# Hybrid encoder trunk: gate and branch products with tokens as the stationary side, 512 weight columns moving

## The reference

```
h = rms_norm(x, norm1_g[l])
(aq, ak, av, bq, ..., c_q, c_kv, k_rope) = split(h @ w_in[l])
...                                              # o_a, o_b, o_c, o_d: four attentions
br = stack([o_a, o_b, o_c, o_d], axis=2)         # 256 channels each
y = einsum('bsnc,ncd->bsnd', br, w_branch[l])
g = sigmoid(h @ w_gate[l] + b_gate[l]).reshape(B, S, 4, D)
x = x + sum(g * y, axis=2) @ w_o[l]
h2 = rms_norm(x, norm2_g[l])
x = x + square(relu(h2 @ w_ff1[l])) @ w_ff2[l]
```

## Time and profile before

| | |
|---|---|
| median of 3 runs | 831.93 us (831.73 to 832.6) |
| profiled execution, its time | 832.6 us |
| its span | 830.8 us |
| TensorE busy | 816.9 us, 5763 products |
| VectorE busy | 544.4 us, 805 instructions |
| ScalarE busy | 409.6 us, 698 instructions |
| GpSimd busy | 45.7 us |
| transfers | 141.09 MB, 170 GB/s on average |
| granted TensorE clock | 1.00 in every slice |

### The profile page before, as it was taken

One profiled execution on the slowest core, in us unless ns is written; L12 is line 12 of the kernel. 1 busy time (PEld: TensorE's weight loads), 2 busy tenths in 40 slices (PEclk: granted clock), 3 DMA queues, 4 the chain that ended last, 5 costly groups with the idle time before them and its releaser, 6 DMA issues.

```text
span 830.8 us, 14799 instructions
## 1 busy us (share of the span) xinstructions
PE 816.9 (98%) x5763; PEld 749.1 (90%) x5763; DVE 544.4 (66%) x805; ACT 409.6 (49%) x698; POOL 45.7 (5%) x81
## 2 busy tenths in 40 slices
PE   7999999999999999999999999999999999999996
PEld 6999979999899999999899999799988999999995
DVE  6687676865776665555767675687665865555663
ACT  6356655655454444333464475575545544333442
POOL 1420000000010000000013100000000100000000
PEclk9999999999999999999999999999999999999999
DMA  8976534536347555566546755334353665566541
GB/s 248 227 233 198 158 120 135 150 105 204 101 156 237 169 174 178 200 202 199 170 128 194 241 167 177 116 102 153 126 177 104 212 199 178 197 202 198 170 137 50
DMA packets 100851, 141.09 MB, mean 170 GB/s; under 512 B 4797, under 2 KB 87041, under 8 KB 100801
## 3 DMA queue, kind: packets, MB, share of 16 engines
q1 hardware_dynamic: 99296, 137.12, 52.1%
q0 software_dynamic: 1216, 3.17, 1.7%
q10 hardware_dynamic: 288, 0.11, 0.1%
HBM read 139.33 MB, written 1.05 MB: 169 GB/s over the span
## 4 chain that ended last, share of the span: by engine, by line
PE 93%; DVE 3%; ACT 1%; issue 1%; POOL 1%; DMA 1%; POOLq 0%; ACTq 0%; DVEq 0%
PE bank_w L1190 20%; PE bank_w L1192 19%; PE bank_w L1191 19%; PE bank_acc L1190 8%; PE bank_acc L1191 8%; PE bank_acc L1192 8%; PE bank_acc L1286 2%; PE bank_o L1315 2%; PE bank_acc L1298 2%; DVE w_lo L810 2%; DMA cst<-in_table 1%; PE bank_x L1263 0%; PE bank_x L1268 0%; POOL rstd L498 0%; PE bank_x L1259 0%
## 5 line engine op out<-in xcount | busy, mean ns | idle before, releaser
L810 DVE TENSOR_TENSOR w_lo<-raw,w_hi 128x1024 fp32r<-128x1024 f32 (+1 forms) x256 | 309.0, 1255 | 49.6 <-ACT w_hi L575 49.5
L1190 PE MATMUL bank_w<-act_hi,w_hi 128*128 128x256 f32 x1008 | 287.9, 286 | 0.0
L1192 PE MATMUL bank_w<-act_hi,w_lo 128*128 128x256 f32 x1008 | 285.8, 283 | 0.0
L1191 PE MATMUL bank_w<-act_lo,w_hi 128*128 128x256 f32 x1008 | 285.2, 283 | 0.0
L575 ACT ACTIVATE w_hi<-raw 128x1024 fp32r<-128x1024 f32 (+1 forms) x256 | 257.0, 1060 | 26.7 <-DMA raw<-in_w_gate 12.9
L1190 PEld LDWEIGHTS bank_w<-act_hi,w_hi 128*128 128x128 f32 x1008 | 191.6, 190 | 6.9 <-ACT big L696 3.5
L1191 PEld LDWEIGHTS bank_w<-act_lo,w_hi 128*128 128x128 f32 x1008 | 190.9, 189 | 1.8 <-issue 0.5
L1192 PEld LDWEIGHTS bank_w<-act_hi,w_lo 128*128 128x128 f32 x1008 | 191.2, 190 | 0.0
L704 ACT ACTIVATE part_hi<-big 128x512 fp32r<-128x512 f32 x32 | 20.3, 633 | 194.2 <-DVE big L1038 191.5
L1190 PE MATMUL bank_acc<-w_hi,part_hi 128*128 128x512 f32 x256 | 100.3, 392 | 0.0
L1191 PE MATMUL bank_acc<-w_lo,part_hi 128*128 128x512 f32 x256 | 100.3, 392 | 0.0
(11 more groups left out here) (180 smaller groups left out, 938.5 us busy)
## 6 DMA issues: line engine op xcount, KB each, us to landing
raw<-in_w_ff SPq DMA_DIRECT2D x128, 512.0 KB, 4.7
raw<-in_w_gate SPq DMA_DIRECT2D x64, 512.0 KB, 4.7
raw<-in_w_in SPq DMA_DIRECT2D x32, 536.0 KB, 5.5
raw<-in_w_o SPq DMA_DIRECT2D x16, 512.0 KB, 4.5
raw<-in_w_branch SPq DMA_DIRECT2D x16, 256.0 KB, 4.5
raw<-in_w_branch SPq DMA_DIRECT2D x8, 512.0 KB, 4.6
xs<-in_x SPq DMA_DIRECT2D x2, 512.0 KB, 4.6
out_y<-big SPq DMA_DIRECT2D x4, 256.0 KB, 2.1
```

The lines of the kernel that those rows point to most:

```text
L810: nc.vector.tensor_tensor(half_view(w_lo, c, hf), raw_half(c, hf), f32(half_view(w_hi, c, hf)), ALU.subtract).then_inc(w_lo_ready, 1)
L1190: nc.tensor.matmul(dst, s_hi, m_hi, start=first, stop=False)
L1191: nc.tensor.matmul(dst, s_hi, m_lo, start=False, stop=False)
L1192: ins = nc.tensor.matmul(dst, s_lo, m_hi, start=False, stop=last)
```

## The change

**Gates.** Two gate chunks form a group of 512 features: chunk 2g holds the first half of the inner dimension, 2g+1 the second. The tokens become the stationary side, and 512 weight columns move. The group takes both banks, one for each half of the tokens; the sums run over both chunks. Gate weights are loaded in rows of 512 columns.

**Bias.** A feature is now a column, so the bias is a row. GpSimd broadcasts 512 biases to all partitions for each group (`gate_row`, two buffers). VectorE adds it from PSUM into `big` (`gate_add`): for the first token half as soon as TensorE's semaphore `gate_first` tells of it in the middle of the odd chunk, for the second at the end of the step. TensorE waits for these additions, and ScalarE's tanh, in `big` itself, comes behind them. The bias columns are gone from `vec_all`.

**Branches.** Quarters are now (token half, 512 features), 6 products of 128x512 each. The first comes behind gate 7 instead of 6, the third behind 13 instead of 12.

**Mixture.** `mix` has tokens on partitions now, so TensorE transposes it (16 transposes of 128x128 a layer), and ScalarE and VectorE read the turned quarters from PSUM. VectorE's split of `w_o` chunk 2 moves behind the last branch.

```diff
-Y_AFTER = {3 * n + 6: n for n in range(NB - 1)}
+Y_AFTER = {7: 0, 9: 1, 13: 2}
+GROUPS = GATE_N // 2
...
@@ SP: loads @@
+                if kind == "gate":
+                    k = KD // 2 * (i % 2) + 2 * h
+                    src = w_gate.rearrange("l (k p) (c n) -> l c p k n", p=P, n=512)[l, i // 2]
+                    sp.dma_start(dst.rearrange("p (k n) -> p k n", k=2), src[:, k:k + 2, :]).then_inc(done, 16)
...
@@ GpSimd @@
+            def gate_bias(l, g):
+                row = b_gate[bass.ds(l, 1), g * 512:(g + 1) * 512]
+                pool.dma_start(gate_row[:, g % 2, :], row.to_broadcast([P, 512])).then_inc(gate_row_landed[g % 2], 16)
...
                 norm(2 * l, l)
+                pool.wait_ge(gate_read, l * GATE_N)
+                for g in range(2):
+                    gate_bias(l, g)
...
+                for g in range(2, GROUPS):
+                    pool.wait_ge(gate_read, l * GATE_N + 2 * (g - 1))
+                    gate_bias(l, g)
                 norm(2 * l + 1, l)
...
@@ ScalarE, gate(i, l) @@
+                g = i // 2
+                if i % 2 == 0:
+                    return
+                for t in range(T):
+                    z = gate_slot(g // 2, 2 * t + g % 2)
+                    act.wait_ge(gate_read, l * GATE_N + (2 * g + t + 1))
+                    nc.scalar.activation(z, z, ACT.Tanh, scale=0.5).then_inc(gate_tanh, 1)
...
@@ VectorE @@
+            def gate_add(i, t, l):
+                g = i // 2
+                if i % 2 == 0:
+                    return
+                if t == 0:
+                    dve.wait_ge(gate_row_landed[g % 2], 16 * (l * GROUPS // 2 + g // 2 + 1))
+                    dve.wait_ge(gate_first, l * GROUPS + (g + 1))
+                else:
+                    dve.wait_ge(w_used, used_count(l, POS["gate", i]))
+                nc.vector.tensor_tensor(gate_slot(g // 2, 2 * t + g % 2), bank_w[:, t, :], gate_row[:, g % 2, :],
+                                        ALU.add).then_inc(gate_read, 1)
...
@@ TensorE @@
-                    pe.wait_ge(gate_tanh, l * GATE_N + (n + 1))
+                    pe.wait_ge(gate_read, l * GATE_N + (2 * n + q + 1))
...
+            def gate(i, l):
+                g, half = divmod(i, 2)
...
+                for t in range(T):
+                    tok = slice(t * P, (t + 1) * P)
+                    if half == 0:
+                        bank_free(("gate", g, t), l)
...
+                    ins = split_product(bank_w[:, t, :], sides, half == 0, half == 1)
+                    if half and t == 0:
+                        ins.then_inc(gate_first, 1)
+                ins.then_inc(w_used, 1)
...
+            def turn_mix(q, l):
+                pe.wait_ge(mixed, l * 12 + (8 + q + 1))
+                for j in range(KD // 2):
+                    ins = nc.tensor.transpose(mix_banks[q][:, j * P:(j + 1) * P], mix[:, q, j * P:(j + 1) * P], ident)
+                ins.then_inc(mix_turned, 1)
+            def last_branch(l):
+                for q in range(3):
+                    branch_part(NB - 1, q, l)
+                turn_mix(0, l)
+                branch_part(NB - 1, 3, l)
+                turn_mix(1, l)
...
@@ w_o_sums @@
+                    if c == 0:
+                        turn_mix(2, l)
+                        turn_mix(3, l)
```

More of the change, by code:

```diff
@@ L75 @@
 W_JOBS = []
-for _i in range(GATE_N):
-    W_JOBS.append(("gate", _i, 0))
-    if _i in Y_AFTER:
-        W_JOBS += [("y", Y_AFTER[_i], q) for q in range(4)]
+for _g in range(GROUPS):
+    W_JOBS += [("gate", _g, t) for t in range(T)]
+    if 2 * _g + 1 in Y_AFTER:
+        W_JOBS += [("y", Y_AFTER[2 * _g + 1], q) for q in range(4)]
 W_JOBS += [("y", NB - 1, q) for q in range(4)]
@@ L315, in trunk_kernel @@
         x_evac = sem("x_evac")
+        gate_row_landed = [sem(f"gate_row_landed{b}") for b in range(2)]
+        gate_first = sem("gate_first")
+        gate_read = sem("gate_read")
         gate_tanh = sem("gate_tanh")
@@ L689, in gate, with mix_hi @@
             def gate(i, l):
-                act.wait_ge(w_used, used_count(l, POS["gate", i]))
-                if i >= 8:
-                    act.wait_ge(y_read, l * 16 + (i - 7))
-                bank = bank_w[:, W_AT["gate", i, 0] % 2, :]
-                for d in range(2):
-                    ins = nc.scalar.activation(big[:, i % 8, d * SEQ:(d + 1) * SEQ], bank[:, d * SEQ:(d + 1) * SEQ],
-                                               ACT.Tanh, bias=vec(BG + 2 * i + d, l), scale=0.5)
-                ins.then_inc(gate_tanh, 1)
+                g = i // 2
[5 more added lines that the diff above has]
+                    nc.scalar.activation(z, z, ACT.Tanh, scale=0.5).then_inc(gate_tanh, 1)
+            def mix_hi(q, l):
+                t, m = divmod(q, 2)
+                kcs = slice(m * KD // 2, (m + 1) * KD // 2)
+                act.wait_ge(mix_turned, l * 4 + (q + 1))
+                nc.scalar.activation(act_hi[:, kcs, t * P:(t + 1) * P], mix_banks[q].rearrange("p (k s) -> p k s", s=P),
+                                     ACT.Copy, scale=0.5).then_inc(mix_hi_ready, 1)
             def mlp(i, l, g=0):
@@ L1075, in _ @@
                         branch(j, l, (0, 1))
+                    if kind == "gate":
+                        gate_add(j, 0, l)
                     if kind == "in":
@@ L1094, in _ @@
                             split_lo(c, l)
+                    if kind == "gate":
+                        gate_add(j, 1, l)
                     if s == 8:
```

86 lines of the change are left out of this document (46 added, 40 removed).

## The result

| | before | after |
|---|---|---|
| median on the same chip, 4 runs each | 832.1 us (831.73 to 832.6) | 847.6 us (846.3 to 849.25) |
| ratio, 95% interval | | 1.0188 (1.0172 to 1.0203) |
| span of the profiled execution | 830.8 us | 846.6 us |
| mean granted TensorE clock | 1.00 | 0.992 |
| products and transposes on TensorE | 5763 | 4835 |

The account below looks back on a forecast made before the run. TensorE, busy 98% of the span, was taken as the bound. Products, transposes and old waits gave -7.2 us, new waits +19.8, bias rows +0.5: +13.1, so 845.0 us on the median, range 833 to 852 for 8 in 10.

Parts of the forecast that it names:

- transposes and excursions: Turning the mixture: 16 transposes a layer, 1.86 us, plus three excursions into and out of small work, 0.6; 4.9 us more.
- place 1: Gate 1 to gate 2: TensorE waits for banks that VectorE's additions free late; 4.5 us lost in each layer.
- place 2: Step 15 to 16: k/v up-projection waits for ScalarE's copy behind the second addition and tanh; 1.8 us lost a layer.
- place 3: Step 18 to 19: first k transposes wait for ScalarE's copy behind late addition and tanh; 2.5 us lost a layer.
- place 4: Gate 13 to branch 2: VectorE reads the first quarter late, TensorE wants its bank for the third; 1.1 us a layer.
- bias rows and head: GpSimd's first two bias broadcasts of layer 0 compete with late weight loads; cost between 0 and 2.3 us, taken as 0.5.
- 40 x 0.28: 16 gate and 4 branch chunks per layer turn wide, each saving the MLP stage's 0.28 us: 11.2 us less.
- The rival that rests on the Trainium skill's figure: Gates and branches: each product saved is worth only 2.5 ns, so the gain is 2.4 us: 853.8; chance 0.02.
- M: End of a step's maxima on VectorE; 75.23 in step 9, with the second addition ending at M + 6.66.
- The covers hold: Rival: the second addition is nowhere wanted before it is done, so no new waits: 824.7 us; chance 0.13.
- only place 1 bites: Rival: queues behind the other three places are shorter than reckoned, only gate 2 waits: 834.2 us; chance 0.15.
- Lateness carries on: Rival: ScalarE's waits delay later work, other group borders lose too, bias rows cost 2.3; waits 26 us: 853; chance 0.15.

Follow-up runs that it names:

- halves beside the split last: 832 of the 960 wide products done as two of 256 columns, against the version with the split last (833.3 us): 840.05 us, ratio 1.0098.
- the split last: VectorE's weight split put behind normalising and second addition in every gate step, against the kernel after the change: 833.32 us, ratio 1.0011 to the kernel before.
- kept-busy run: 24 identity transposes on TensorE during its wait before gate 2's second token half, against the kernel after the change: 843.06 us, ratio 1.0127.
- tuned version: Against the split last: step 9's first addition and branch 1's first two reads ahead of maxima, `w_o` chunk 1's split behind the last branch: 843.65 us.
- additions in a row: VectorE's second addition straight behind the first, split and normalising after both, against the kernel after the change: 836.93 us, ratio 1.0058.
- transposes doubled beside the tuned version: Each of the mixture's 32 transposes done twice, against the tuned version: 843.85 us, ratio 1.0138.
- short rows: Each half chunk of gate weights loaded as two loads of 256 columns (1 KB pieces), against the kernel after the change: 847.52 us, ratio 1.0176.

## Why the prediction was right

The direction, the place and the mechanism held: 847.6 lies in the forecast's own 840 to 850, and the waits are at the four places named. Moving the second addition takes back nearly all of the loss, and moving only the copies takes back the share of places 2 and 3. The size is in part luck: the total is closer than its terms, which missed in both directions. Without the half clock, which the forecast did not have, it would have been near 843.

| term | forecast | shown | by |
|---|---|---|---|
| products, 960 fewer | -11.2 | -7.4 (-7.8 to -8.8) | lengths of chunks (halves beside the split last) |
| transposes and excursions | +4.9 | +3.3 | rows after; 0.103 us each when doubled |
| old waits | -0.9 | -0.9 | waits after |
| place 1, two layers | +9.0 | +7.7 | waits after |
| place 2 | +3.6 | +2.8 | waits after |
| place 3 | +5.0 | +3.7 | waits after |
| place 4 | +2.2 | +0.7 | waits after |
| waits beyond their listed lengths | none | +1.6 | start to start, old waits taken off |
| bias rows and head | +0.5 | -0.5 | start of gate 0 |
| half clock | none | +4.8 | clock after; kept-busy run |

With -7.4 the shown terms add up to +15.8 (places 1 to 4: 14.9), with the halves' -7.8 to -8.8 to +14.4 to +15.4; the spans differ by 15.8.

- **Products: mis-sized.** The step that failed is "40 x 0.28": it took the saving of a wide chunk from the MLP and set it into the gate stage. There the wide form's pitch is 2% longer in every odd step, and a gate chunk saves 0.19 us on average, a branch chunk 0.15. The rival that rests on the Trainium skill's figure (2.4 us) is further off: the measured value is 8.1 to 9.2 ns a product, 7.7 by the lengths of the chunks.
- **Transposes: mis-sized.** The 0.6 us a layer for "three excursions" were an allowance; the rows after show 0.1 at most.
- **Waits: the mechanism right, each a little smaller.** In step 9 M came at 74.25, not 75.23; the term counted the step from M with 6.66 us, and 6.57 were measured. The place was put at 4.5 a layer, and was 4.1 and 3.6. The reason given for an earlier M, the 2 KB rows, fell in an experiment. At place 2 the second addition came when forecast (8.7 us after the gate's start, 8.75 forecast), but TensorE, whose chunk was longer than reckoned, wanted the bank 0.25 us later; at place 4 it was 0.45 later. So the error of the products made some of these waits smaller.
- **The clock: a missing term.** The forecast reckoned a wait of TensorE at its own length. Two of the waits (2.97 and 2.94 us), and one of 1.42, cost 1.6 us more each, nearly a third of the whole loss. No row of the kernel before could show it, since nothing there waits so long once TensorE is running.
- **The covers hold** (0.13) fell by the 14.9 us of waits, and **only place 1 bites** (0.15) by the 7.2 us at the other three. **Lateness carries on** (0.15): the other group borders lost nothing, and 14.9 us is far from its 26. That its 853 is nearer than 834 comes from the clock, not from its mechanism.
- **The bias rows** cost nothing: gate 0 starts 0.48 us earlier than before. Whether that comes from the removed bias columns or elsewhere was not tried. In the profiled runs of the edited kernels, none of which changes the head, it starts between 59.9 and 60.7, so some of the 0.48 is scatter.

Of the smaller experiments' forecasts five clearly missed as well. The version with the split last kept 5.3 us of waits, not 2, and the tuned version's rival took over, as did the rivals of the additions in a row and of the transposes doubled beside the tuned version; the short rows changed nothing. In the first two a VectorE item was moved by looking at who waits for it, and not at who waits for what it now delays.

## What to carry to other kernels

When a bank's reader moves from one engine to another, find its place in the new engine's queue and count what stands ahead of it: here 0.7 us of work behind 4 us of splits and normalising cost more than 960 saved products gave. The cure is an order, not fewer instructions: what frees a bank goes ahead of what has slack, here splits that run three chunks ahead. Price an idle time of TensorE of about 3 us at its length plus what the clock may take behind it, and take the price of a product from the stage where it will run.

## What the runs showed of the hardware

- The profiled runs of seven of these kernels have 14 waits of TensorE of 2.94 to 3.94 us in the gate stages. Around the end of 13 of them the granted clock fell to one half, from 1.7 us before TensorE restarted to 1.4 us after it, and stayed there for 3.4 us (ten times) or 6.8 us (three times). The pitch of 128x512 products is 0.427 us then instead of 0.23. The one without a fall is in layer 0 of the run with short rows (2.95 us). With small transposes in the same gap, in both layers of one run, the clock did not fall.
- Shorter waits had it too, and seldom: in the three profiled runs that have both waits in both layers the clock fell behind the wait of 1.42 us for the up-projection's bank once in six, and behind the wait of 1.86 us for the k transposes once in six.
- Two narrow products (256 columns) of the fast type take 0.240 us, one wide product 0.228 us in the MLP stage and in the even steps of the gate stage, and 0.232 to 0.233 in its odd steps. Behind small products the first of either form has 0.1 us more to the next.
- Loads of a weight chunk in pieces of 1 KB or 2 KB landed about equally early in the stage where they were late (ScalarE began on them at 67.99 and 68.28 us).
